# A two-layer mixer and mixture-of-experts trunk: weight splits, waits and banks moved around TensorE's waits

## The reference

```
h = layer_norm(x)                                   # once, ahead of the layers
z = h @ w_in[l]                                     # 8012 columns: queries, keys, values of three branches, gates
o_diff = differential attention (4 heads x 2)       # rotary q and k, chunk mask
o_dsa  = sparse attention (8 heads)                 # an indexer's scores pick the keys that a query keeps
o_fox  = forgetting attention (8 heads)             # causal, with summed log forget gates, no rotation
y = sum over the branches of sigmoid(gate_b) * (o_b @ w_br[b])
h = layer_norm(alpha * h + y @ w_o)                 # "ln1"
h = layer_norm(alpha * h + experts(h))              # "ln2": 32 SwiGLU experts, two of them for each token
```

## Time and profile before

| what | value |
|---|---|
| median of three runs | 2194.59 us (2194.47 to 2197.5) |
| the profiled execution's own time | 2194.75 us |
| its span, first to last instruction | 2193.0 us |
| mean granted TensorE clock | 0.975 of full speed |
| TensorE matmul busy | 1998.4 us (91%) |
| VectorE busy | 956.9 us (44%) |
| ScalarE busy | 673.2 us (31%) |
| GpSimd busy | 206.4 us (9%) |
| chain that ended last, by engine | PE 76%, DMA 9%, DVE 6%, issue 3% |

### The profile page before, as it was taken

The page is one execution under the profiler, slowest core; times in us unless marked ns, Lnnn a source line. Parts: engine busy times, 40 slices in busy tenths (PEclk is TensorE's granted clock), DMA queues, the critical chain, the costliest instruction groups (busy, mean ns, idle before and its releaser), DMA issues.

```text
span 2193.0 us, 30522 instructions
## 1 busy us (share of the span) xinstructions
PE 1998.4 (91%) x10004; PEld 1222.2 (56%) x10012; DVE 956.9 (44%) x1898; ACT 673.2 (31%) x1358; POOL 206.4 (9%) x244
## 2 busy tenths in 40 slices
PE   6999999999979987888899999999998999878887
PEld 5777777877733332222377787777777333222232
DVE  5766865846641111111257667656665311110113
ACT  3554555546110000000144536646550000000000
POOL 3000002000111111111000000110001111111100
PEclk9999999999989999999999999999999999999998
DMA  5321321323789999999942123123158899999996
GB/s 175 119 74 40 116 78 39 116 78 135 295 328 422 425 425 426 425 426 420 380 142 77 40 77 116 40 77 116 40 200 318 349 423 426 425 426 425 426 419 265
DMA packets 104248, 535.63 MB, mean 244 GB/s; under 512 B 14848, under 2 KB 17792, under 8 KB 83600
## 3 DMA queue, kind: packets, MB, share of 16 engines
q1 hardware_dynamic: 92112, 510.41, 58.0%
q0 software_dynamic: 11968, 23.11, 2.8%
HBM read 527.17 MB, written 23.07 MB: 251 GB/s over the span
## 4 chain that ended last, share of the span: by engine, by line
PE 76%; DMA 9%; DVE 6%; issue 3%; another core or an unknown queue 2%; SPq 1%; ACT 1%; DVEq 0%; POOL 0%; POOLq 0%; ACTq 0%
PE ps L1208 17%; PE ps L846 12%; PE ps L848 12%; PE ps L847 12%; PE ps L1228 8%; DMA wslot<-in_w_up 4%; PE ps L967 3%; DMA scr<-in_w_up 2%; PE ps L997 2%; PE ps L1028 2%; PE ps L1198 1%; DVE scr L2326 1%; DMA h<-h_rows 1%; PE ps L1021 1%
## 5 line engine op out<-in xcount | busy, mean ns | idle before, releaser
L2306 DVE COPY scr<-ps 128x512 f32<-128x512 f32 x64 | 44.3, 692 | 729.0 <-PE ps L1198 728.9
L846 PE MATMUL ps<-hT_lo,w_hi 128*128 128x512 f32 (+1 forms) x816 | 327.2, 401 | 5.7 <-DVE w_lo L1751 5.7
L848 PE MATMUL ps<-hT_hi,w_hi 128*128 128x512 f32 (+1 forms) x816 | 318.8, 391 | 0.0
L847 PE MATMUL ps<-hT_hi,w_lo 128*128 128x512 f32 (+1 forms) x816 | 318.0, 390 | 0.0
L1391 ACT ACTIVATE scr<-ps 128x512 f32<-128x512 f32 (+1 forms) x214 | 111.3, 524 | 546.9 <-PE ps L1228 308.8
L1209 PE MATMUL ps<-scr 128*64 128x512 f32 x480 | 228.5, 632 | 0.0
L1228 PE MATMUL ps<-ring,scr 128*64 128x512 f32 x736 | 168.1, 598 | 33.4 <-DVE scr L2326 33.4
L1687 ACT ACTIVATE scr<-ps 64x512 f32<-64x512 f32 x64 | 37.7, 590 | 508.1 <-PE ps L1209 508.1
L1751 DVE TENSOR_TENSOR w_lo<-ring,w_hi 128x1024 fp32r<-128x1024 f32 x114 | 139.3, 1222 | 84.9 <-ACT w_hi L1411 79.1
L846 PEld LDWEIGHTS ps<-hT_lo,w_hi 128*128 128x128 f32 (+1 forms) x816 | 153.1, 188 | 37.8 <-issue 6.9
L848 PEld LDWEIGHTS ps<-hT_hi,w_hi 128*128 128x128 f32 (+1 forms) x816 | 152.8, 187 | 33.4
(11 more groups left out here) (269 smaller groups left out, 3322.9 us busy)
## 6 DMA issues: line engine op xcount, KB each, us to landing
ring<-in_w_down SPq DMA_DIRECT2D x42, 2048.0 KB, 46.7
ring<-in_w_in SPq DMA_DIRECT2D x29, 2048.0 KB, 7.8
scr<-in_w_up SPq DMA_DIRECT2D x26, 2048.0 KB, 50.3
xslot<-in_w_up SPq DMA_DIRECT2D x14, 2048.0 KB, 43.0
spare<-in_w_gate SPq DMA_DIRECT2D x14, 2048.0 KB, 47.1
ring<-in_w_gate SPq DMA_DIRECT2D x12, 2048.0 KB, 43.1
scr<-in_w_gate SPq DMA_DIRECT2D x12, 2048.0 KB, 44.5
h<-in_w_gate SPq DMA_DIRECT2D x12, 2048.0 KB, 45.7
```

The lines of the kernel that those rows point to most:

```text
L846: mm(out, a[0], b[1], start=first, stop=False)
L847: mm(out, a[1], b[0], start=False, stop=False)
L848: return mm(out, a[0], b[0], start=False, stop=last)
```

## The change

Seven edits, and one condition that goes with them.

1. On ScalarE and VectorE, the split of the fourth query unit of `d` and `s` is put ahead of all rotations of the branch.
2. TensorE's wait for the value blocks is taken from the start of the attention to just ahead of their first use, in turn 1.
3. The last key block of `f` goes to bank 5.
4. Widening block 4 of `d` goes to bank 6, as that of `s` did, and its first three quarters are done after the transposes of the last normed steps; `gated_sum` reads it there.
5. In turn 7, VectorE makes the last low part of `w_br` where the next unit's split stood, and that split moves to the end of the turn.
6. In the output, half 0, tiles 0 and 1 are interleaved: blocks 0 to 5 of tile 0, blocks 0 to 5 of tile 1, blocks 6 and 7 of tile 0, blocks 6 and 7 of tile 1.
7. The last multiply-add of tile 3 of `ln1` is cut into two halves, and TensorE's transposes of the first half wait for the first alone.

```
         def br_bank(br, c):
-            return 6 if (br, c) == (BRANCHES[-1], 4) else c % 4
+            return 6 if br != BRANCHES[0] and c == 4 else c % 4
...
                 def transpose_tile(key, t, l=0):
-                    pe.wait_ge(h_ready.sem, h_ready.at((key, t), l))
+                    pe.wait_ge(h_ready.sem, h_ready.at((key, t, 0) if (key, t) == ("ln1", NT - 1) else (key, t), l))
                     for half in range(2):
+                        if half and (key, t) == ("ln1", NT - 1):
+                            pe.wait_ge(h_ready.sem, h_ready.at((key, t), l))
...
-                            project(key, l, name, n)
+                            project(key, l, name, n, 5 if key == ("fk", KB - 1) else None)
...
-                    for t in range(NT):
-                        if br == "f":
-                            b = c_bank(t, 0)
-                            pe.wait_ge(bank[b].read, bank[b].full.start(l))
-                        else:
-                            in_sbuf(book.where[(br + "v", t)], (br + "v", t), l)
+                    def values_in_sbuf():
+                        for t in range(NT):
+                            if br == "f":
+                                b = c_bank(t, 0)
+                                pe.wait_ge(bank[b].read, bank[b].full.start(l))
+                            else:
+                                in_sbuf(book.where[(br + "v", t)], (br + "v", t), l)
...
+                        if m == 1:
+                            values_in_sbuf()
                         if m >= 1:
                             for n in before:
                                 values(n)
                     if br != "s":
                         after = BRANCHES[BRANCHES.index(br) + 1] + "q"
                         project((after, 0), l, after, 0, 4)
-                    else:
-                        widen(br, 4, range(KB - 1), l)
                     if br == "d":
                         for n in (NSTEP - 2, NSTEP - 1):
                             turn_normed(n)
+                    if br != "f":
+                        widen(br, 4, range(KB - 1), l)
...
+                    def products(t, half, blocks):
+                        if blocks[0] == 0:
+                            free(4 + t, l)
+                        for k in blocks:
+                            if t == 0:
+                                pe.wait_ge(wo_ready.sem, wo_ready.at((half, k), l))
+                                alone(pe)
+                            if t == 0 and half == 0:
+                                pe.wait_ge(y_ready.sem, y_ready.at(("y", k), l))
+                                alone(pe)
+                            ins = product(t, half, k)
+                        if blocks[-1] == KD - 1:
+                            filled(ins, 4 + t, ("m", t, half))
+
+                    for blocks in (range(KD - 2), range(KD - 2, KD)):
+                        for t in range(2):
+                            products(t, 0, blocks)
                     for half in range(2):
                         for t in range(NT):
-                            free(4 + t, l)
-                            for k in range(KD):
-                                if t == 0:
-                                    pe.wait_ge(wo_ready.sem, wo_ready.at((half, k), l))
-                                    alone(pe)
-                                if t == 0 and half == 0:
-                                    pe.wait_ge(y_ready.sem, y_ready.at(("y", k), l))
-                                    alone(pe)
-                                ins = product(t, half, k)
-                            filled(ins, 4 + t, ("m", t, half))
+                            if half or t >= 2:
+                                products(t, half, range(KD))
...
                 def take_projections(br, l):              # ScalarE
                     if br != "f":
+                        split_to((br + "q", 3), l)
                         for c in (KD - 2, KD - 1):
...
                                                                # VectorE, normalise
-                    V.scalar_tensor_tensor(h[:, t, :], h[:, t, :], rstd[:, t:t + 1], ln_params[key][1],
-                                           ALU.mult, ALU.add).then_inc(h_ready.sem, h_ready.tick((key, t)))
+                    cuts = [slice(0, 512), slice(512, D)] if (key, t) == ("ln1", NT - 1) else [slice(0, D)]
+                    for n, cut in enumerate(cuts):
+                        V.scalar_tensor_tensor(h[:, t, cut], h[:, t, cut], rstd[:, t:t + 1], ln_params[key][1][:, cut],
+                                               ALU.mult, ALU.add).then_inc(
+                            h_ready.sem, h_ready.tick((key, t) if n == len(cuts) - 1 else (key, t, 0)))
...
                                                                # VectorE, attention
-                        if 1 <= m < NDUO:
+                        if m - 1 == BR_AT[-1]:
+                            low_branch_weight(KB - 1)
+                        elif 1 <= m:
                             split_to(units[first + min(m + 1, KD - 1 if br == "s" else KD)], l)
                         if m < NDUO:
                             normalise(now[1])
-                        if m - 1 in BR_AT:
+                        if m - 1 in BR_AT[:-1]:
                             low_branch_weight(BR_AT.index(m - 1))
+                        if m == NDUO - 1:
+                            split_to(units[first + (KD - 1 if br == "s" else KD)], l)
...
                 def gated_sum(br, l):
-                        b = c % 4
+                        b = br_bank(br, c)
...
                     for br_ in BRANCHES:                       # VectorE
                         if br_ != "f":
+                            split_to((br_ + "q", 3), l)
```

## The result

| | before | after |
|---|---|---|
| median, us | 2195.72 (2194.47 to 2197.5, 4 runs) | 2173.91 (2172.24 to 2175.91, 4 runs) |
| ratio | | 0.990, 95% interval 0.9883 to 0.9918 |
| profiled execution, us | 2194.75 | 2175.91 |
| its span, us | 2193.0 | 2174.1 |
| matmul busy, us | 1998.4 | 1991.9 |

The forecast was 2176.2 us in a range of 2169 to 2187. The profiled executions are 18.84 us apart, where the sum said 18.4.

What follows compares the result with a forecast made beforehand. TensorE's waits in the mixers were taken as the bound, the weight stream starting anew from TensorE's clock. Terms 0 + 1.7 + 2.1 + 1.1 + 4.3 + 0 = 9.2 us a layer, 18.4 off 2194.6: 2176.2 us, range 2169 to 2187.

Steps and rivals of the forecast that it cites:

- Rival D: Whole layer: the weight stream's start does not move with TensorE, all is taken back, 2194.6 us; chance 0.04.
- signs of being wrong: Split waits at more than one block of a branch, no new key-block waits, or a longer expert stage.
- The last key block of `f`: f's scores: the wait moves from the first duo to the second, gain 0 (bounds 0 and 0.8 us).
- Rival A: Whole kernel: every wait goes and none comes back, 13.2 us a layer, 2168.2 us; chance 0.11.
- The fourth query split in `d`: d's projections: the 2.8 us wait goes, the first key split is late next; gain 1.7 us a layer.
- The value waits: First scores of d and s: 1.0 us gained in each, 2.1 a layer with the wait's own latency.
- Turn 7 and the end of `d`: d's tail into s: 3.0 us gained, a new 1.9 us wait at s's first key block, 1.1 remains.
- Rival C: Blocks after the fourth query block: VectorE's lag recurs at five further blocks, 16.5 us a layer, 2209 us; chance 0.04.
- The output: Output tiles 0 and 1 interleaved: waits on y's low parts go, clock stays full; gain 4.3 us a layer.
- Rival B: Only the output pays, earlier arrivals in the branches become waits on VectorE; 2 x 4.3 us, 2186.0 us; chance 0.16.
- rival E: Output: the first 48 matmuls stay at half clock, 22.1 instead of 11.1 us, 2198.2 us in all; chance 0.02.

Runs made afterwards that it cites:

- branch_end_only: The kernel before with only d's widening block 4 in bank 6 behind the last transposes and turn 7's last low branch weight made earlier; 2189.97 us, ratio 0.997.
- split_first_d_alone: The changed kernel with the fourth query split ahead of the rotations kept in d and taken back in s; 2168.78 us, ratio 0.9873.
- edit1_only: The kernel before with only the fourth query split put ahead of all rotations, in both d and s; 2193.13 us, ratio 0.9985.
- fk_bank_only: The kernel before with only f's last key block put in bank 5; 2196.98 us, ratio 1.000.

## Why the prediction was right

**The reading of what bounds the kernel held.** TensorE's waits in the mixers were the path, and what a mixer saved the layer saved: 9.6 and 9.7 us of mixer, 9.1 us at the first expert's matmul, 19.2 at the second layer's. Rival D (no change, the weight stream sets the end) is out. One of the signs of being wrong that the prediction names did appear: the expert stage is longer than before, by 1.25 us and by 0.5. No run ties it to the edits: two profiles of one kernel are 2.0 us apart in the first layer's experts.

**The last key block of `f`, predicted 0.** It gave 0.4 in the ledger, 0.3 of it ahead of the place that the prediction read, and the cause of those 0.3 is open; they are most of what the mixers gained beyond the sum. Alone it gave a ratio of 1.000, since `d`'s fourth query block took all but 0.1 back. The wait went to the second duo, 0.64 us at 122.25. Rival A, every wait goes, is out here and at both key blocks.

**The fourth query split in `d`, 1.7 predicted, 1.8 measured.** The split began at 228.63, where the prediction had 228.62, and the key split began at 239.26, predicted for about 239.4. The engines' order by hand, added up row by row, gave the end of a chain of 11 us to a few tenths. The new wait is 1.14 us, where 1.4 was foretold.

**The value waits, 2.1 predicted, 1.8 measured** in the ledger (0.8 and 1.0) and 2.2 alone, with half-clock time taken off.

**Turn 7 and the end of `d`, 1.1 predicted, 1.2 measured** (3.2 less 2.0). This was the step with the most working, a gain of 3.0 that becomes a new wait of 1.9. The wait is there with 1.70 us, at the first key block and at no other, and branch_end_only and split_first_d_alone show both halves of it apart. Rival C, that the lag comes again at each block, needed waits at more than one block; there are four in the whole span, one in `d` and one in `s` of each layer. ScalarE's copies did stand behind the waiting split: the split begins at 389.99, when the block that began at 384.35 is used, 5.6 us later, the copies follow it, and without this edit in `s` the mixers are 2.0 and 1.9 us shorter. The Trainium skill's "PSUM — Partial Sum Buffer", section "Engine vs sequencer instructions", has ScalarE's queue as strict first in, first out, and this trace agrees.

**The output, 4.3 predicted, 4.3 measured.** Rival B, that only the output pays, would have needed 525.5 to be 531; rival E, that its clock stays low, a clock under 1.00, and it is 1.00. That a mixer of before had just one half-clock stretch, and at the output, is what the one trace showed; the size of this term is in part luck. With the same two waits, edit1_only has no stretch in the mixer of layer one at all.

**Where the prediction was short.** The sum took 18.4 us off 2194.6; the medians moved 21.8. Of the 3.4 us between, 1.1 are that the median of before is 2195.72 with a fourth run and not 2194.59. The profiled pair is only 18.84 us apart, 3.0 less than the medians: the profiled execution of before is 1.0 below its median, and that of after, 2175.91, is the slowest of its four and 2.0 above. In the mixers, 0.4 us a layer is edit 3, put at nothing.

The working priced each half-clock stretch of the mixers that its one trace had, the two at the output, and no other. The experiments' profiles show such stretches behind `d`'s split wait and the branch weights' wait as well, which that trace by chance had not; where they fall, an execution of before is longer by up to 1.7 us each, and after has not those waits. This fits the sign and the size, and fits edit1_only, whose median fell 3.7 us though its mixers, with half-clock time taken off, are no shorter. Each execution's mean granted clock over the whole span is on record, and agrees: it is 0.9734 in the mean of the 20 runs of before in the first set, 0.9761 in that of edit1_only's 11, 0.9772 in that of after's four, and the profiled execution of before had 0.975. An estimate from the first two: 0.0027 x 2195 = 5.9 us less time lost to the lower level, the most that it can be worth, since time lost while the weight stream sets the pace costs nothing. Where in the span the clock fell, only the profiled executions tell, so that the mixers' stretches make the difference of the medians is likely and not shown.

## What to carry to other kernels

Price a removed wait by what is late next, not by its length: write out the chain of each engine in its order from the rows, and ask for every instruction that is moved ahead what now stands behind its wait. The same edit gained 1.8 us in one branch and cost 2.0 in the next, since in one the unit came free before the rotation's copies could begin and in the other it held them up; try such an edit at each place by itself. Filler work, as the rounds of picks, may stand anywhere but ahead of an instruction that a full engine is about to want: spreading six rounds otherwise over four turns made each mixer 1.6 us shorter.

## What the runs showed of the hardware

After a wait of 1 to 3 us between dense matmuls, TensorE's granted clock fell to its 1.2 GHz level for 3.4 us, at times 6.8, in some executions and not in others with the same waits (0.67 and 1.00 over the same five microseconds). A single profile thus misprices a kernel with such waits: fk_bank_only's showed a mixer of 539.2 us against 535.1, and its median was that of the kernel before.
